# One stage of a five-stage software pipeline split into two streams, with markers that hold a PSUM bank, and a smaller waiting penalty in the kernel's own scheduler

## What is computed

```python
a = rmsnorm(h, norm_mix)
z = a @ w_in                                   # 1024 -> 3080 columns
u, vg, q, k, vm, o, zi, zf = split(z)
u = gelu(u); vg = layernorm(gelu(vg), gm_ln_g, gm_ln_b)
y_gm = u * (W_s @ vg + b)                      # per head, causal 128x128
ig = zi + ml_b_i; lf = log_sigmoid(zf + ml_b_f)
# mLSTM, chunk of 128 tokens, per head:
b = cumsum(lf); g = b + m
D = b[:, None] - b[None, :] + ig[None, :]      # masked causal
m_t = maximum(g, max(D, -1))                   # running-max stabiliser
s = (q @ k.T) * exp(D - m_t)
num = s @ v + exp(g - m_t) * (q @ C);  den = sum(s) + exp(g - m_t) * (q @ n)
hm = num / maximum(abs(den), exp(-m_t))
C = exp(g_last - m_new) * C + k.T @ (w_end * v)
h = h + concat(y_gm, sigmoid(o) * rmsnorm(hm)) @ w_out
h = h + square(relu(rmsnorm(h) @ w_up)) @ w_down
h = h + sigmoid(rmsnorm(h) @ w_ple_gate) * (p @ w_ple_proj)
```

## Time and profile before

| | us |
|---|---|
| all runs shown | 1335.98 and 1465.61, median 1400.8 |
| the profiled execution | 1337.89 |
| its span, slowest core (6) | 1336.3 |
| spans of the 8 cores | 1325.6 to 1336.3 |
| TensorE matmuls busy | 985.3 (74%) |
| VectorE, ScalarE, GpSimd busy | 613.3, 439.7, 330.7 |

### The profile page before, as it was taken

The page is one execution under the profiler, slowest core; times in us unless marked ns, Lnnn a source line. Parts: engine busy times, 40 slices in busy tenths (PEclk is TensorE's granted clock), DMA queues, the critical chain, the costliest instruction groups (busy, mean ns, idle before and its releaser), DMA issues.

```text
span 1336.3 us, 16796 instructions; the slowest of 8 cores (1325.6 to 1336.3 us)
## 1 busy us (share of the span) xinstructions
PE 985.3 (74%) x5157; PEld 473.6 (35%) x5252; DVE 613.3 (46%) x1461; ACT 439.7 (33%) x941; POOL 330.7 (25%) x512
## 2 busy tenths in 40 slices
PE   0277887765379988999887487788445998999875
PEld 0133443432134534444433243344212444444432
DVE  1025666554335643333346245665542433333355
ACT  1125453442251201111265354554324211111264
POOL 3114445343131210000223033453522000000032
PEclk9978898886689999999988698898666999999987
DMA  6970005116287763500298500000746982500012
GB/s 121 221 115 1 1 10 49 16 19 107 63 113 156 121 149 40 88 1 1 33 182 171 170 1 1 1 1 1 116 30 73 145 126 36 91 1 1 12 64 83
DMA packets 82762, 91.28 MB, mean 68 GB/s; under 512 B 14450, under 2 KB 64754, under 8 KB 82674
## 3 DMA queue, kind: packets, MB, share of 16 engines
q0 software_dynamic: 53760, 61.90, 30.9%
q1 hardware_dynamic: 28914, 28.29, 8.2%
HBM read 133.96 MB, written 13.93 MB: 111 GB/s over the span
## 4 chain that ended last, share of the span: by engine, by line
PE 55%; DVE 11%; DMA 9%; ACT 8%; issue 8%; POOL 8%; SPq 1%; DVEq 0%; ACTq 0%; POOLq 0%
PE pb L323 52%; ACT AR L421 7%; DMA AR<-w_in 5%; DVE AR L425 4%; POOL AR L425 3%; PE pb L330 3%; POOL SMALL L425 2%; DVE AR L440 2%; DVE SMALL L425 2%; DMA AR<-sC 2%; DMA o_Cs<-AR 1%; DMA AR<-pp 1%; POOL SMALL L433 1%; POOL AR L310 1%; DVE CST L440 1%
## 5 line engine op out<-in xcount | busy, mean ns | idle before, releaser
L323 PE MATMUL pb<-AR 128*128 128x512 bf16 (+3 forms) x4116 | 892.9, 371 | 100.6 <-DVE AR L425 58.4
L323 PEld LDWEIGHTS pb<-AR 128*128 128x128 bf16 x4196 | 393.5, 102 | 551.2 <-issue 197.0
L421 ACT ACTIVATE AR<-pb 128x512 f32<-128x512 f32 (+4 forms) x347 | 187.3, 553 | 516.6 <-PE pb L323 454.9
L425 DVE TENSOR_TENSOR H<-H,pb 128x512 f32<-128x512 f32 x170 | 116.8, 687 | 198.7 <-PE pb L323 190.2
L330 PE MATMUL pb<-IDB,AR 128*128 128x128 bf16 x722 | 84.2, 246 | 147.0 <-ACT AR L421 91.0
L425 DVE TENSOR_TENSOR AR<-AR 128x512 bf16<-128x512 f32 (+3 forms) x180 | 113.1, 632 | 158.6 <-ACT AR L421 157.9
L433 POOL TENSOR_SCALAR SMALL<-SMALL 128x1 f32<-128x1 f32 (+1 forms) x102 | 23.8, 233 | 413.1 <-ACT AR L421 346.9
L330 PEld LDWEIGHTS pb<-IDB,AR 128*128 128x128 bf16 x722 | 58.6, 112 | 185.9 <-issue 177.2
L421 ACT ACTIVATE AR<-H 128x1024 bf16<-128x1024 f32 x68 | 71.6, 1053 | 115.9 <-POOL SMALL L462 66.0
L425 DVE TENSOR_TENSOR AR<-pb,GN 128x1024 bf16<-128x1024 bf16 x51 | 62.2, 1220 | 85.3 <-PE pb L330 85.3
L425 POOL TENSOR_TENSOR AR<-IDB,SMALLB 128x1024 bf16<-128x1024 bf16 x34 | 68.5, 2014 | 86.2 <-DVE SMALL L447 41.8
(11 more groups left out here) (75 smaller groups left out, 533.2 us busy)
## 6 DMA issues: line engine op xcount, KB each, us to landing
AR<-w_up POOLq DMA_DIRECT2D x16, 1024.0 KB, 16.2
AR<-w_down POOLq DMA_DIRECT2D x16, 1024.0 KB, 24.1
AR<-w_in POOLq DMA_DIRECT2D x12, 1024.0 KB, 30.9
y_p<-AR SPq DMA_DIRECT2D x16, 512.0 KB, 2.9
H<-xp SPq DMA_DIRECT2D x9, 512.0 KB, 10.3
AR<-w_out POOLq DMA_DIRECT2D x2, 2048.0 KB, 55.4
AR<-sC SPq DMA_DIRECT2D x8, 512.0 KB, 4.4
AR<-w_pg POOLq DMA_DIRECT2D x2, 2048.0 KB, 17.6
```

What stands on the lines that cost most here:

```text
L323: ins = e.matmul(out, l, r, start=(i == 0), stop=(i == n - 1))
L421: return S.op("act", lambda e: e.activation(out=out, in_=in_, func=func, **kw), aps(in_, bias, scale), aps(out, accum))
L425: return S.op(eng, lambda e: e.tensor_tensor(out=out, in0=in0, in1=in1, op=op), [in0, in1], [out])
```

## The change

`stage_P1` is cut in two. The parts (1) to (4) stay in it; the parts (5) and (6), which need nothing of them, become `stage_P1b`, a stream of its own that runs in the same iteration and for the same tile. Since both write bank 4, and a bank is handed on from one piece of work to the next by order alone, each such piece is now bracketed by `mark("begin", bank)` and `mark("end", bank)`; while one stream holds a bank, `run_streams` does not take the other's `begin`. The sample tile's loads of `NCOL` and of three of the state's heads are now issued in `stage_P1`, behind part (4). `run_pipeline` takes stages with an offset each, so that two can share one. `PE_WAIT_MARGIN` goes from 3.5 to 2.0, for all phases. No instruction is added or removed by the change itself; ScalarE's table loads are put in later, where the order of its functions asks for them.

```diff
-PE_WAIT_MARGIN = 3.5
+PE_WAIT_MARGIN = 2.0
...
+    def mark(self, kind, bank):
+        if self.capture is not None:
+            self.capture.append(("bank", kind, bank, None, None, 0.0))
...
     def run_streams(self, streams):
         ptr = [0] * len(streams)
+        holder = {}
         while True:
             best = None
             for i, stm in enumerate(streams):
-                if ptr[i] >= len(stm):
+                blocked = False
+                while ptr[i] < len(stm) and stm[ptr[i]][0] == "bank":
+                    _, mk, bank_, _, _, _ = stm[ptr[i]]
+                    if mk == "begin":
+                        if holder.get(bank_) not in (None, i):
+                            blocked = True
+                            break
+                        holder[bank_] = i
+                    else:
+                        holder[bank_] = None
+                    ptr[i] += 1
+                if blocked or ptr[i] >= len(stm):
                     continue
...
                 bt = bP.next()
+                S.mark("begin", bt)
...
                 cp("dve", KT[d2], PBB[bt][:, 512:1024].rearrange("p (h t) -> p h t", h=4))
+                S.mark("end", bt)
                 yield
...
                 cp("act", YT[d3][:, 0:4, :], PBB[by][:, 0:512].rearrange("p (k t) -> p k t", k=4))
-                yield
+                S.mark("end", by)
+                if ty == 1:
+                    S.dma(NCOL[:], snT.rearrange("h d j -> d h j"))
+                    for h in range(3):
+                        S.dma(CSB3[h][:, :, 0:128], sC[:, h, :, :].rearrange("j d e -> d j e"), eng="pool")
+                yield
+
+            def stage_P1b(t):
+                ty = t["ty"]; g = t["g"]; d2 = g % 2; d3 = g % 3; d4 = g % 4
+                sm = lambda off, n: small(g % 5, off, n)
+                zg = sm(4, 8)
+                bP = bP1
                 ig = sm(24, 4); e1 = sm(28, 4); l1 = sm(32, 4); bb = sm(36, 4); aa = sm(44, 4)
...
                 bc = bP.next()
+                S.mark("begin", bc)
                 ps_c = PB[bc][:, 0:4]
                 S.mm(ps_c, [(CM[:, CM_CUM + ty, :], l1)])
                 ts("dve", bb, ps_c, -1.0, ALU.mult)
+                S.mark("end", bc)
...
-            run_pipeline(sg, [stage_N, stage_P, stage_P1, stage_M1, stage_M2],
+            run_pipeline(sg, [(0, stage_N), (1, stage_P), (2, stage_P1), (2, stage_P1b), (3, stage_M1),
+                              (4, stage_M2)],
```

More of the change, by code:

```diff
@@ L578, in run_pipeline @@
             n = len(tiles)
-            for it in range(n + len(stages) - 1):
+            stages = [st_ if isinstance(st_, tuple) else (k_, st_) for k_, st_ in enumerate(stages)]
+            max_off = max(o_ for o_, _ in stages)
+            for it in range(n + max_off):
                 streams = []
-                for s_i in reversed(range(len(stages))):
-                    ti = it - s_i
+                for (off_, fn_) in sorted(stages, key=lambda x: -x[0]):
+                    ti = it - off_
                     if 0 <= ti < n:
                         S.capture = []
-                        for _ in stages[s_i](tiles[ti]):
+                        for _ in fn_(tiles[ti]):
                             pass
@@ L591, in run_pipeline @@
                     for o in stm:
-                        busy[o[1]] = busy.get(o[1], 0.0) + o[5]
+                        if o[0] != "bank":
+                            busy[o[1]] = busy.get(o[1], 0.0) + o[5]
                 if background is not None and it in background and background[it] is not None:
@@ L772, in stage_P1 @@
                 bs_ = bP.next()
+                S.mark("begin", bs_)
                 ps_s = PB[bs_][:, :]
@@ L778, in stage_P1 @@
                         GN[:, GN_BS + ty * 4 + h:GN_BS + ty * 4 + h + 1], U_[:, h * 128:(h + 1) * 128], ALU.add, ALU.mult)
+                S.mark("end", bs_)
                 yield
                 by = bP.next()
+                S.mark("begin", by)
                 for h in range(4):
@@ L797, in stage_P1 @@
                 ba = bP.next()
+                S.mark("begin", ba)
                 ps_A = PB[ba][:, :]
@@ L801, in stage_P1 @@
                    CM[:, CM_MASK + ty, :].unsqueeze(1).to_broadcast([128, 4, 128]), ALU.add)
+                S.mark("end", ba)
                 redmax(mx, PBIG)
                 tt("dve", mx, mx, bb, ALU.add)
[L804 to L807, removed]
                 yield
```

## The result

The changed kernel takes 1345.03 us (median of 32 runs) against 1341.77 of the kernel before (31 runs beside them): the ratio of the two is 1.0034, with a 95% interval of 1.0025 to 1.0043. It is 0.3% slower. In some executions of either kernel the cores of one die run longer at a lower granted clock; every ratio here leaves these out (without them the medians are 1344.5 and 1340.0). I had forecast 1317 us, 1.5% faster, with 1341 as the high end of the range. The profiled execution took 1346.3 us, its slowest core (core 1) 1344.7.

What follows compares the result with a forecast made beforehand. It took TensorE to bound the kernel, busy 985.3 of 1336.3 us, with time to win in phase A. Gains of 2.7 + 12 + 5.9 = 20.6 us off 1337.9 gave 1317 us, range 1298 to 1341.

Steps and rivals of the forecast that it cites:

- Ramps: First P1 iteration of each phase A: 4.25 us of waiting go, less a 1.31 us table load; 5.9 us gained together.
- Drains: Last iterations of each phase A: TensorE's waits go until M2's chain binds; 6 us gained each, 12 us together.
- Table loads: ScalarE, gates' Exp and Ln between two tiles' Gelus: four more set changes, loads rising from 33 to about 37.
- Full iterations: Nine phase A iterations with all stages: broadcast wait goes, M2's chain comes next; 0.3 us gained each, 2.7 us together.
- P1's product of 2.35 us: GpSimd's product for P1's broadcast, moved under TensorE's groups: costs 0, however long it takes there.
- The margin: Margin of 2.0 reorders phase C's transposes among its groups: 0, between 2 us gained and 2 lost.
- B: Rival: at full iterations' passage, two new waits and another clock fall cost 3.5 us each; 1351 us, chance 0.08.
- C: Rival: waits in drains and ramps are only renamed, other stages binding; 0 to 5 us gained, 1335 us, chance 0.16.
- A: Rival: the passage between phase A iterations is really freed, 4.29 us in each full iteration; 1281 us, chance 0.12.

Runs made afterwards that it cites:

- the split alone: The changed kernel with PE_WAIT_MARGIN back at 3.5 instead of 2.0: 0.9937 of the kernel before, 8.4 us faster.
- the emptied kernels: Changed kernel and kernel before with GpSimd's two products and layer-norm gain and bias cut to 4 columns, memsets filling their time: 0.9857 and 0.9896 of before.

## Why the prediction was wrong

*Ramps: 5.9 us.* Right in sign, a little small: the first tiles come 3.1 and 4.5 us sooner (7.6; 10.0 with the split alone). The wait of 3.06 us became one of 2.35, so the gain is not where I had put it:

```profile
788.10 0.59 PE L339 MATMUL pb<-AR,ONESB 128*128 128x512 bf16 x2 [2.35 <-POOL SMALL L478]
```

*Drains: 12 us.* The last two intervals, which I had at 2 x 3.6 us, gave 4.7 + 5.9 = 10.6. The first drain iteration, which I took to gain 2.35 us in each group, lost: 27.1 to 28.7 and 27.3 to 28.9 us, and TensorE waits 6.84 us in it. Together 7.4 us for 12.

*Table loads.* 37, as counted.

*Full iterations: 2.7 us gained, at worst 0.9 lost in each.* This is the term that failed: the 22.3 us lost less the 3.2 of the first drain iterations are 19.1 us, 2.1 lost in each of nine where I had 0.3 gained. It has two parts, which the emptied kernels tell apart. 13.4 us of it are there without these holds. I had taken all that stands behind the state update to move 0.6 us earlier with the product gone; instead, at the passage shown, P1's layer norm came in between M2's Squares and its power (3.71 us for 1.34), TensorE waits 2.50 us for `YML` with the reads gone, and the clock falls behind that wait. The other part, some 5.7 us here and 6 in the first drain iterations, is the line "P1's product of 2.35 us stands under TensorE's groups at its new place, however long it takes there: 0". It does stand under TensorE's groups. It also stands on VectorE, which is held by it, and by the layer norm's operations next to it, while it makes what TensorE waits for next. Before, TensorE waited there for the product itself, which took 2.35 us where others take 1.89, so holds cost something there too (13.9 us in the whole kernel), but less. I asked what the moved instruction delays on its own queue and who waits for its result, and neither what comes into the awaited chain in its stead nor whose instructions it lengthens.

One reading was wrong besides: the row of ScalarE at 889.10, `AR<-H` 128x1024, is `stage_N`'s Square and not one of M2's, which follow behind it (`AR<-AR` 128x128, from 890.16). The Squares stand in ScalarE's queue behind it, so the chain runs as I followed it; its first Square only starts 1.06 us later than I had it.

*The margin: 0, between 2 us gained and 2 lost.* Wrong too: 1.0% on top of the split, some 13 us; 5 or 6 of them in the second C, the rest in phases A through the holds. I had weighed it as an edit by itself, where it costs 0.2%.

*The rivals.* B was the nearest, in its place and in its sign: the mean spacing of the nine full passages rose from 26.2 to 28.3 us (in the second group from 24.7 to 27.3, over the 25.5 that was its sign), and its point of decision, a second wait over 2 us, is met in two of the four full passages of the second group (4.90 and 2.22 us; 1.13 and 0.59 in the others) and in the first drain iteration (7.84). I had priced it at 3.5 us in every iteration, where 2.1 came, and given it 0.08. Its reason, a second wait and a second fall of the clock, is what is left with the reads emptied; the holds, which it did not have, come on top. C's condition, phases A within 3 us of the old length, is met as well, but not by renamed waits: gains and losses of 10 us cancel. A was excluded by the `YML` waits, as argued.

With these four reads per tile gone the split is worth 1.0% (0.9796 against 0.9896), 13.4 us; with them 8.4; with them and the margin of 2.0 the kernel is 4.5 us slower than before. The 20.6 us of the forecast would have been 7 too many even so, because at the freed passages A^T and `YML` are late without these holds too (1.15 and 2.50 us of waiting in the emptied kernel).

## What to carry to other kernels

When a stage is moved, see what of it now stands inside the chain that TensorE awaits. When an instruction of GpSimd that reads SBUF is moved, look at what VectorE does at the new place, and whether TensorE waits for that; the same hold costs nothing under work that nobody awaits. If an engine's busy time changes while its instruction count does not, compare the mean durations by shape before looking at any wait. Measure a tuning number again after the code that it was tuned with has changed, and each alone: here the margin cost 0.2% on one version and 1.0% on the other.

## What the runs showed of the hardware

An operation on 4 columns of VectorE took 0.16 us beside memsets of GpSimd and 1.77 us beside a product of 1.89. Over the whole changed kernel the reads of four operations per tile on GpSimd cost 24 us, 1.8% of the time, and in the kernel before 14 us. GpSimd's addition of 128x512 writes bf16 from f32 inputs in 1.32 us on average, where the one that writes f32 takes 1.34 with the split alone, so that the cast of 0.72 us per tile behind it can be left out. A fused operation of VectorE on 128x512 with two inputs in SBUF took 0.91 us on average against 1.34 for one of GpSimd in the split alone, and using it made the kernel slower.
